# Attention with sinks: a tile's scaled output is turned one tile later on PE and copied one step later on DVE

## The reference, cut to what matters

```python
def sliding_window_attention(q, k, v, sinks):
    ...
    kb, vb = banded(k), banded(v)
    s = jnp.einsum('bnqkgd,bnjkd->bnkgqj', qb, kb, preferred_element_type=jnp.float32) * scale
    ...
    s = jnp.where(mask[None, :, None, None], s, -jnp.inf)
    ...
    p = jax.nn.softmax(jnp.concatenate([s, sink], axis=-1), axis=-1)[..., :-1]
    o = jnp.einsum('bnkgqj,bnjkd->bnqkgd', p.astype(v.dtype), vb)
    return o.reshape(B, S, H, D)

mix = jnp.concatenate([fox_out, swa_out], axis=-1) @ w_out[l]
```

## Time and profile before

| | us |
|---|---|
| median of 3 runs | 2947.18 (2940.68 to 2950.18) |
| the profiled execution | 2942.5 |
| its span, first to last instruction | 2940.7 |
| busy over the span: PE, DVE | 2642.6 (90%), 2408.1 (82%) |
| busy over the span: ACT, POOL | 867.9 (30%), 1319.5 (45%) |
| the stretch of attention with sinks | 396 to 553 |
| flips (L262) in it | 32, of 64 in the program |

### The profile page before, as it was taken

How to read it: one execution, slowest core, us unless ns; L and a number is a source line. 1 busy time by engine, 2 the same in 40 slices (tenths; PEclk the granted TensorE clock), 3 DMA queues, 4 the chain that set the end, 5 groups by cost and what they waited for, 6 DMA issues and landing times. The chain is left out here.

```text
span 2940.7 us, 46951 instructions
## 1 busy us (share of the span) xinstructions
PE 2642.6 (90%) x17459; PEld 1721.0 (59%) x17459; DVE 2408.1 (82%) x4501; ACT 867.9 (30%) x1463; POOL 1319.5 (45%) x869
## 2 busy tenths in 40 slices
PE   8999888798867765699999999999999999999996
PEld 3566655458867764455555555555555555555552
DVE  3244555574999998489999999999999999999998
ACT  2333333211114555422222222222222222222223
POOL 2110000210014442046666666666677767766772
PEclk9999989799978885799999999999999999999998
DMA  4000010261002243789999999999999999999994
GB/s 155 23 15 15 15 72 15 88 250 51 1 1 115 114 163 150 287 293 354 359 351 357 364 347 361 362 353 368 324 339 347 346 344 348 332 354 339 340 337 170
DMA packets 262958, 685.24 MB, mean 233 GB/s; under 512 B 35624, under 2 KB 118184, under 8 KB 258352
## 3 DMA queue, kind: packets, MB, share of 16 engines
q0 software_dynamic: 110592, 402.70, 36.8%
q1 hardware_dynamic: 152240, 280.98, 27.4%
HBM read 624.89 MB, written 58.72 MB: 232 GB/s over the span
## 5 line engine op out<-in xcount | busy, mean ns | idle before, releaser
L1886 PE MATMUL h_psum<-early 128*128 128x384 bf16 (+1 forms) x6144 | 859.2, 300 | 23.4 <-issue 12.7
L1904 PE MATMUL o_psum<-v_split,w_split 128*128 128x512 bf16 x3840 | 856.7, 381 | 20.1 <-DVE wide L1745 20.0
L1886 PEld LDWEIGHTS h_psum<-early 128*128 128x128 bf16 x6144 | 602.6, 98 | 279.4 <-issue 26.6
L1904 PEld LDWEIGHTS o_psum<-v_split,w_split 128*128 128x128 bf16 x3840 | 375.5, 98 | 461.4 <-DVE wide L1745 25.3
L1701 POOL DMA_INDIRECT early<-v_blocks,pick_index x320 | 486.2, 1520 | 200.7 <-DVE wide L1757 119.1
L1701 POOL DMA_INDIRECT early<-u_rows,pick_index x320 | 426.4, 1333 | 329.5 <-DVE dots L1753 214.8
L1757 DVE SCALAR_TENSOR_TENSOR wide<-early,dots,wide 128x1024 f32<-128x1024 f32 x320 | 399.4, 1281 | 34.0 <-DMA early<-v_blocks,pick_index 33.3
L1753 DVE CUSTOM_DVE_ANT_0 early<-early,wide 128x1024 f32<-128x1024 f32 x320 | 380.7, 1220 | 25.5 <-DMA early<-u_rows,pick_index 24.6
L1648 ACT ACTIVATE w_split<-act_out 128x640 bf16<-128x640 f32 x128 | 94.3, 737 | 706.1 <-DVE act_out L1721 648.4
L1635 ACT ACTIVATE act_out<-h_psum 128x384 f32<-128x384 f32 (+1 forms) x256 | 97.2, 431 | 522.5 <-PE h_psum L1886 479.7
L1110 PE MATMUL r_t_psum<-rt_x_t,early 128*128 128x128 f32 (+1 forms) x1920 | 234.6, 283 | 0.0
(11 more groups left out here) (202 smaller groups left out, 2961.2 us busy)
## 6 DMA issues: line engine op xcount, KB each, us to landing
early<-u_blocks SPq DMA_DIRECT2D x128, 512.0 KB
early<-v_blocks SPq DMA_DIRECT2D x128, 512.0 KB
gates<-wide SPq DMA_DIRECT2D x20, 2048.0 KB, 6.3
gate<-gates SPq DMA_DIRECT2D x32, 1280.0 KB
early<-w_query SPq DMA_DIRECT2D x8, 1024.0 KB, 5.9
att_w_raw<-w_fox SPq DMA_DIRECT2D x4, 1536.0 KB, 7.0
early<-u_rows,pick_index POOLq DMA_INDIRECT x320
early<-v_blocks,pick_index POOLq DMA_INDIRECT x320
```

Source lines behind the costliest of these rows:

```text
L1886: mm = pe.matmul(h_psum[k][:, half, 0:width * P], u_split[:, k, part, c], xs[:, first:first + width, xpart, c, :], start=(c == 0 and part ...
L1904: mm = pe.matmul(o_psum[(DENSE * p + t) % 2][:, half * 512:half * 512 + 512], w_split[:, p, q, part, t * P:(t + 1) * P], v_split[:, p, q, ...
```

## The change

On PE the flip moves from the end of a step to behind its scores, ahead of the first half of the projection, and is that of tile qb-2 instead of qb-1. On DVE the copies move from behind the scaling of tile qb-1 to ahead of it, behind the maxima, and are those of tile qb-2. The first steps of a pair finish the last two tiles of the pair before, and behind the last pair one more flip and copy are written out. No instruction is added or removed, and no wait is changed; which tile a wait stands for follows from the tile's number.

```diff
--- before.py
+++ after.py
@@ -447,6 +447,10 @@
                             sw_score(pair, kp, qb + 2)
                         elif not last:
                             sw_score(pair + 1, 1 - kp, qb + 2 - TILES)
+                        if qb >= 2:
+                            sw_flip(pair, qb - 2)
+                        elif past(pair):
+                            sw_flip(pair - 1, TILES - 2 + qb)
                         share = 0 if last else SWA_SHARES[qb]
                         if share:
                             project_swa(pair + 1, 1 - kp, done, done + share // 2)
@@ -458,11 +462,8 @@
                         if share:
                             project_swa(pair + 1, 1 - kp, done + share // 2, done + share)
                         done += share
-                        if qb >= 1:
-                            sw_flip(pair, qb - 1)
-                        elif past(pair):
-                            sw_flip(pair - 1, TILES - 1)
                     if last:
+                        sw_flip(pair, TILES - 2)
                         sw_values(pair, TILES - 1)
                         sw_flip(pair, TILES - 1)
 
@@ -625,17 +626,18 @@
                             maxima(pair, qb + 1)
                         elif not last:
                             maxima(pair + 1, 0)
+                        if qb >= 2:
+                            copy_flipped(PAIRS + pair, kp, qb - 2, stored)
+                        elif past(pair):
+                            copy_flipped(PAIRS + pair - 1, 1 - kp, TILES - 2 + qb, 0)
                         if qb >= 1:
                             sw_scale_out(pair, qb - 1)
                         elif past(pair):
                             sw_scale_out(pair - 1, TILES - 1)
-                        if qb >= 1:
-                            copy_flipped(PAIRS + pair, kp, qb - 1, stored)
-                        elif past(pair):
-                            copy_flipped(PAIRS + pair - 1, 1 - kp, TILES - 1, 0)
                         if not last and qb in SWA_ROTATED:
                             rope(pair + 1, 1 - kp, SWA_ROTATED.index(qb))
                     if last:
+                        copy_flipped(PAIRS + pair, kp, TILES - 2, 0)
                         sw_scale_out(pair, TILES - 1)
                         copy_flipped(PAIRS + pair, kp, TILES - 1, 0)
```

## The result

| | before | after |
|---|---|---|
| median (us) | 2947.39 (2940.68 to 2950.22, 7 runs) | 2958.96 (2951.80 to 2962.17, 7 runs) |
| the profiled execution | 2942.5 | 2954.98 |
| its span | 2940.7 | 2953.2 |
| first scores of the stage to end of its last copy | 395.96 to 552.78: 156.8 | 400.57 to 569.13: 168.6 |

The ratio of after to before is 1.0035, with a 95% interval of 1.0019 to 1.0051: **the change makes the kernel about 10 us slower**. The time lies 7.6 us above the forecast of 2951.4, 2 us beyond the forecast's own range (2946 to 2957) and 1 us inside the wide one (2938 to 2960), at the price of the third rival, the clock that falls a step sooner (2956.5 to 2959). The prediction called up to 0.3% the same and gave that 0.80; the measured 0.35% is just beyond, with 0.3% inside its interval, on the side that had 0.10.

What follows compares the result with a forecast made beforehand. The prediction took DVE to bound the late steps of a pair, and a ring through POOL the last pair. Its terms, 2.0 - 0.7 + 0.6 + 2.3 = +4.2 us, gave a median of 2951.4 us, own range 2946 to 2957, wide range 2938 to 2960.

Steps and rivals of the forecast that it cites:

- the third rival: Clock falls a step sooner, before step 5's rotation: 2956.5 us, or 2959 if also low half a projection longer; chance 0.13.
- steps 0 to 3 of pairs 0, 1, 2: Steps carrying projection work: half a projection, some 1.3 us, covers the copy, so they cost nothing.
- pair 0, steps 4 to 7: Escaping POOL's delay of L600 in step 4 wins 1.7 us, less the usual 1.0 lost: -0.7 us.
- pair 1: Steps 4 to 7, likewise in pair 2: values wait for copies; each pair loses 1.0 us, +2.0 for both.
- last pair up to the last maxima: POOL's w_out split still sets the pitch; L600 held every time, some three steps at +0.2: +0.6 us.
- its end: Last pair's end: three rounds of values, scaling, flip, copy remain after copy 4: 12.1 us for 9.8, +2.3 us.
- The predicted ring: Rope steps 4 and 5: values wait for the older tile's copy, scaling for values; pitch about 5.6 us instead of 4.81.
- The walk of a pair: Steps 4 to 7 laid out on measured pitches at full clock: next pair's scores start at 16.97 us.
- The hold: Pair 0, step 4: L600, held 2.00 us beside POOL's L665, goes free and L611 is held instead; wins 1.7 us.
- the second rival: The clock stays up as PE's waits move elsewhere: -7.8 us, 2939.4; chance 0.12.
- The first rival: PE's wait at the flip simply goes, some 13 us won, if values never wait for the copy: 2934 us; chance 0.07.
- One sign: In the changed kernel's profile, the stage's last copy ends between -2 and +9 us of 552.8 (+4.2).

Runs made afterwards that it cites:

- e2_dve_only: Kernel before with only DVE's half of the change (copies behind the maxima, a tile older), PE's flip left at the step's end: 2961.3 us, ratio 1.0039.
- e4_filled: Changed kernel with the turns done five times in steps 5 and 6, and in steps 1 to 7 of the last pair: 2947.3 us, ratio 0.9995.
- the filled kernels: e4_filled and e6_before_filled: new and old order, each with added PE work where PE waits; 2947.3 and 2942.9 us.
- e10: Changed kernel unaltered, one further execution for a second profile: stage 168.3 us, against 168.6 in its first profile.
- e5_last_pair_old: Changed kernel with the last pair put back in the old order on PE and DVE: 2960.2 us, ratio 1.0043.
- e3_own_bank: Changed kernel with the flip written to unused columns of the scores' buffers, so values wait for no copy: 2931.1 us, ratio 0.9942.
- e6_before_filled: Kernel before with unread transposes added in steps 5 and 6, and in steps 1 to 7 of the last pair: 2942.9 us, ratio 0.9983.

## Why the prediction was right in kind and short by 7.6 us

The sum of the prediction against the two traces, each pair from its step 4 scores to the next pair's:

| term | forecast | measured |
|---|---|---|
| steps 0 to 3 of pairs 0, 1, 2 | 0 | +0.4, +1.4, +0.2 |
| pair 0, steps 4 to 7 | -0.7 | +2.7 (19.1 to 21.8) |
| pair 1 | +1.0 | +2.5 (17.4 to 19.9) |
| pair 2 | +1.0 | +1.8 (17.9 to 19.7) |
| last pair up to the last maxima | +0.6 | +0.5 (30.7 to 31.3) |
| its end | +2.3 | +2.3 (9.8 to 12.0) |
| sum | +4.2 | +11.7 |

- **What bounds the stage: right.** DVE's full row made PE's wait at the flip worthless. The predicted ring (copy, values, scaling, rotation, rope, maxima) is in the rows of after and e2_dve_only: 25.9 us of L435 for about 20 said, a rope pitch of 5.71 for 5.6, 2.3 us left at L262.
- **The walk of a pair: right at full clock.** It put the values of step 6 at 13.21 behind the scores of step 4; after shows 478.86 - 465.50 = 13.36, and in e4_filled 472.61 - 459.25 is 13.36 again. The handover from copy to values is the 0.15 assumed (472.71 + 0.29 to 473.15). Steps 4 to 7 take 17.34 us in e4_filled (459.25 to 476.59) for 16.97 laid out: a values run that has waited takes 1.00 us to the next scores, not 0.84.
- **Pair 0: the mechanism right, the term wrong.** The hold did leave L600 for L611 (0.16 and 1.76 us), as the Trainium skill (SBUF — State Buffer, SBUF: two separate sides) has it for any VectorE operation with two SBUF inputs beside a GpSimd one that reads SBUF. But the gain assumed that the rest of the pair went as in the others, and it went at the low clock from step 5 on. The gain was also too large: in the filled kernels, both at full clock, the pair takes 17.53 us against 17.50, and pairs 1 and 2 take 17.34 and 17.35 against 16.03, so a pair loses 1.3 and not 0.9, and the hold was worth 1.3 and not 1.7.
- **The step that failed is the one on the clock.** The prediction took step 7 to be low as before and nothing else, +1.5 us on 16.97, and gave 0.13 to a fall one step sooner. It fell behind the wait of step 5 in pair 0, as the third rival described it for all three, and behind that of step 6 in pairs 1 and 2, before the values, where the forecast had only step 7 low. The evidence was in the text: two waits of 2.4 and 2.7 us were laid out in neighbouring steps where before had 1.33 and 2.44, and the fall was known to follow such waits. It was used in full against the second rival, and for the third only up to its 0.13. The filled kernels give its size: 6.6 of the 11.7 us as measured, 8 to 9 by the estimate above. That the rest lies near the 4.2 forecast is in part luck, as the terms of pair 0 and of the pairs 1 and 2 were each off in the order's own share, too.
- **Steps 0 to 3 are not free**: they took 2.0 us more, mostly in pair 1 (1.4), whose first steps inherit pair 0's low clock (0.50 up to 447); in e10, where they did not, they took no more than before.
- **Last pair and end: sized right** (0.5 and 2.3), though L601 was not held in every step: at 531.69 it took 0.34. e5_last_pair_old, which should have shown that by taking them back, did not, so they rest on the two timelines alone.
- **The first rival** (the wait simply goes) needed the values not to wait for the copy. That is what e3_own_bank makes true; it came out at 2931.1 for the 2934 written there, partly by another way: DVE's row became 0.5 us shorter per rope step, too. **The second** (the clock stays up) is what e4_filled forces, and it gave 2947.3, not 2939.4. Its stage is 1.9 us shorter than before's, not 7.8. The last pair took 42.3 us for 40.5, where the rival had 1.8 less (2.4 of that is the filling's); pair 1's start was at full speed in before already, so that its 1.5 was not there to win (19.1 us in both); and steps 4 to 7 of pairs 0 and 1 gave 1.6 and 0.1 for 2.1 and 0.4.
- One sign was missed: the last copy ended 16.3 us later than before, not within 9; 4.6 of that lie ahead of the stage.

What stays open: why the clock falls in step 5 in one pair and in step 6 in another of the same kernel (after, e10), what the end of the last pair costs at full clock without a filling in its way, and whether the two terms of the last pair would be given back at a full clock.

## What to carry to other kernels

When an engine waits for one that is full, moving its work elsewhere may only change which row the wait stands in; look for what the moved handover now holds back, above all a buffer in a shared bank. A cross-engine handover has two ends and a buffer: here moving either end, or both, lost 11 us of the stage, moving only the buffer away from the values gave nothing, and moving both ends and the buffer won 0.6% of the kernel's time. Where a stretch is lightly loaded on TensorE, price the idle time that an edit adds twice, once as waiting and once at the lower clock of what follows.

## What the runs showed of the hardware that was not expected

- Work that nobody needs can pay for itself: 184 added transposes raised the stage's granted clock from 0.86 to 0.98 and took 7 us off it (e6_before_filled), and in the new order 13.7 us (0.80 to 0.96, e4_filled).
- The granted clock differs between executions of one kernel at the same place (step 5 or 6 of pair 1 in after and e10), and so does the start of the unchanged stage, by some 5 us (0.89 and 0.79 from 350 to 396 us in the two profiles of before), while the length of the stage repeats within 0.5.
- VectorE's small operations with both inputs in SBUF were held beside POOL for 1.76 us (L612), 1.61 to 2.02 (L601) and 0.84 to 1.89 (L604 and L615 in e3_own_bank's last pair), and in no row shown here one that reads PSUM.
